# Issuing the down weights of the sorted experts from ScalarE instead of SyncE

## The reference

```
sel = exp_logits[group with the largest logit]        # 8 experts
ev, ei = top_k(softmax(sel), 2);  weights = group_p * ev / sum(ev)
for e in range(32):
    hid = silu(t @ w_expert_gate[e]) * (t @ w_expert_up[e])     # 1024 -> 256
    out = out + combine[:, e:e+1] * (hid @ w_expert_down[e])    # 256 -> 1024
return rms_norm(x + out, final_norm_gain)
```

## Time and profile before

| | us |
|---|---|
| median of 3 runs | 773.46 (772.38 to 773.94) |
| profiled execution | 772.11 |
| its span | 770.4 |
| PE busy | 698.3 (91%) |
| ACT busy | 289.1 (38%) |
| chain that ended last: PE | 83% |

### The profile page before, as it was taken

The page is one execution under the profiler, slowest core; times in us unless marked ns, Lnnn a source line. Parts: engine busy times, 40 slices in busy tenths (PEclk is TensorE's granted clock), DMA queues, the critical chain, the costliest instruction groups (busy, mean ns, idle before and its releaser), DMA issues.

```text
span 770.4 us, 10976 instructions
## 1 busy us (share of the span) xinstructions
PE 698.3 (91%) x4246; PEld 512.1 (66%) x4246; DVE 335.0 (43%) x614; ACT 289.1 (38%) x534; POOL 199.7 (26%) x171
## 2 busy tenths in 40 slices
PE   3999999998999999999999995699999999997840
PEld 3688888887878798888777885454454555554420
DVE  4349897979684423465478136500000000000008
ACT  6313645571444653555543032021222223131203
POOL 2045433431241231542452000212212121221110
PEclk9999999999999999999999996699999999999975
DMA  7913333030030030205841339999999999999726
GB/s 228 353 57 135 110 110 109 15 137 14 28 124 14 2 111 1 110 1 213 333 145 57 131 119 393 367 381 397 419 400 418 397 419 400 418 419 419 304 93 251
DMA packets 45122, 164.66 MB, mean 214 GB/s; under 512 B 9420, under 2 KB 13532, under 8 KB 32270
## 3 DMA queue, kind: packets, MB, share of 16 engines
q1 hardware_dynamic: 39758, 155.52, 52.1%
q0 software_dynamic: 5312, 8.42, 3.1%
HBM read 154.09 MB, written 19.53 MB: 225 GB/s over the span
## 4 chain that ended last, share of the span: by engine, by line
PE 83%; DVE 6%; ACT 4%; issue 3%; DMA 2%; POOL 1%; POOLq 0%; ACTq 0%; DVEq 0%
PE bank L970 14%; PE bank L472 13%; PE bank L474 13%; PE bank L473 13%; PE bank L1004 7%; PE bank L967 5%; PE bank L945 3%; PE bank L998 2%; PE bank L600 2%; PE bank L981 2%; DVE arena L2383 1%; PE bank L863 1%; PE bank L631 1%; PE bank L621 1%; PE bank L803 1%
## 5 line engine op out<-in xcount | busy, mean ns | idle before, releaser
L1258 POOL TENSOR_TENSOR w_lo<-arena,w_hi 128x1024 fp32r<-128x1024 f32 x36 | 86.0, 2395 | 209.4 <-ACT w_hi L1421 209.4
L472 PE MATMUL bank<-h_hi,w_hi 128*128 128x512 f32 x320 | 128.2, 401 | 0.4 <-DVE arena L1970 0.4
L474 PE MATMUL bank<-h_hi,w_lo 128*128 128x512 f32 x320 | 124.9, 390 | 0.0
L473 PE MATMUL bank<-h_lo,w_hi 128*128 128x512 f32 x320 | 124.6, 390 | 0.0
L970 PE MATMUL bank<-arena 128*64 128x256 f32 x896 | 107.1, 394 | 8.2 <-issue 7.4
L970 PEld LDWEIGHTS bank<-arena 128*64 128x64 f32 x896 | 66.5, 141 | 38.8 <-issue 8.6
L2337 DVE TENSOR_TENSOR arena<-arena,bank 64x256 f32<-64x256 f32 x28 | 11.6, 413 | 181.8 <-ACT arena L1772 181.8
L1882 DVE SCALAR_TENSOR_TENSOR bank<-arena,bank 128x512 f32<-128x512 f32 x116 | 78.7, 749 | 0.1
L1382 POOL DMA_INDIRECT y_rows<-arena,row_half x28 | 28.1, 1002 | 166.8 <-ACT arena L1793 155.5
L474 PEld LDWEIGHTS bank<-h_hi,w_lo 128*128 128x128 f32 x320 | 60.0, 188 | 13.1
L472 PEld LDWEIGHTS bank<-h_hi,w_hi 128*128 128x128 f32 x320 | 60.1, 188 | 12.9 <-DVE arena L1970 0.6
(11 more groups left out here) (358 smaller groups left out, 1128.2 us busy)
## 6 DMA issues: line engine op xcount, KB each, us to landing
arena<-in_w_expert_down_dram SPq DMA_DIRECT2D x33, 1024.0 KB
arena<-in_w_expert_gate_dram SPq DMA_DIRECT2D x33, 1024.0 KB
arena<-in_w_expert_up_dram SPq DMA_DIRECT2D x33, 1024.0 KB
arena<-in_w_in_dram SPq DMA_DIRECT2D x8, 2048.0 KB, 8.2
arena<-in_x_dram SPq DMA_DIRECT2D x8, 512.0 KB, 7.3
arena<-in_w_in_dram SPq DMA_DIRECT2D x4, 1024.0 KB, 10.3
y_rows<-arena SPq DMA_DIRECT2D x8, 512.0 KB, 10.4
arena<-in_w_out_dram SPq DMA_DIRECT2D x2, 2048.0 KB, 10.5
```

The source lines that it names most:

```text
L472: pe.matmul(o, wh, xh, start=first, stop=False)
L473: pe.matmul(o, wh, xl, start=False, stop=False)
L474: return pe.matmul(o, wl, xh, start=False, stop=last)
L1258: gp.tensor_tensor(as_raw(w_lo[pslot(s)], s), raw(s), as_raw(w_hi[pslot(s)], s).bitcast(F32), ALU.subtract)\
```

## The change

SP keeps the issue of gate and up and no longer waits for `ex_d`. The down weights of steps 6 to 32 are issued by ACT: in step i, behind the copy of the rows `ex_y(i - 1)`, it reads the expert's number of step i + 5 from `order_i` and issues that step's down weights on its own queue. `ex_y(i - 1)` has waited for the down matmuls of step i - 1, whose slot is overwritten.

```
-                wait(sp, "ex_d", outs(i))
-                expert_dn(s, e)
...
+            def down_load(s):
+
+                o = 0 if s == EXTRA else col_of[s]
+                e = act.value_load(order_i[0:1, o:o + 1], min_val=0, max_val=NE - 1)
+                act.dma_start(wd[slot_of(s)], a["w_expert_down"][0].rearrange("e (p m) n -> e p m n", m=JE)[e])\
+                    .then_inc(S[f"ld_d{slot_of(s)}"], 16)
...
                 if i > 0:
                     ex_y(i - 1)
+                    if i - 1 + NSLOT < NSTEP:
+                        down_load(steps[i - 1 + NSLOT])
```

## The result

The changed kernel takes 775.87 us in the median of 16 runs (773.45 to 779.7), the kernel before 773.23 us in as many. The ratio is 1.0053 with a 95% interval of 1.0039 to 1.0067: slower by 3.0 to 5.2 us, while the two medians lie 2.6 us apart. I had forecast +4.7 us. One run of the kernel before, at 837.25 us, was in a slow state of the chip and is left out of the ratio.

A forecast was written before the change was run, and what follows sets the result against it. DMA was taken to bound the tail. Four downs ahead (10.0 us) less 0.5 early gain delay steps 28 and 29; step 32's matmuls end at 741.4, not 736.71: +4.7 us, 776.8 (778.2 on the runs' scale), range 772.0 to 782.0.

The forecast's parts named there:

- The bytes and not the issue bound the tail: Steps 28 to 32: landing depends on bytes queued ahead, 2.50 us per down, not on when a transfer is issued.
- A second queue is served beside the first: ACT's queue takes turns with SP's, so a down lands a few us after issue while SP's gate and up wait.
- Four downs come ahead of gate and up: Steps 28 and 29: four downs newly ahead, 4 x 2.50 us less 0.5, landing at 709.1 and 717.6.
- early gain: Between 500 and 512 us, where the queue ran dry: gate and up issued sooner win 0.5 us, bounds 0 and 0.7.
- PE cannot catch up: After a 2.7 us wait before step 29, PE starts step 32 from work at 737.8, its matmuls taking 3.60 us.
- ACT's work is hidden: Between ex_y and hidT_copy: 0.8 us a step, 22 us in 27 steps, cost 0; without DMA cover 0.7 us.
- Rival C: ACT's issues of downs are held by the backlog, making hidT_copy late: 4 us on top, 782; chance 0.12.
- Rival A: DMA engines serve both queues by age, gate and up one down further ahead: gain 3.0 us, 770.5; chance 0.12.
- Rival B: Step 32's late landing is paid back by the clock, 1.76 us; +0.2 to +0.9 remain, 773.7 to 774.4; chance 0.18.

The follow-up runs named there:

- e6: Against the kernel before, ACT issues only the downs of steps 6 to 18, SP those of steps 19 to 32: 0.9968, -2.5 us.
- e8: Against the kernel before, SP issues the downs of steps 6 to 18, ACT those of steps 19 to 32: 1.0046, +3.6 us.
- e3: The changed kernel, but in step i ACT issues the down of step i + 3, not i + 5: 1.0048 against the kernel before, +3.7 us.
- e7: The changed kernel with ACT's lead five steps for the downs of steps 6 to 8, then three: 1.0030 against the kernel before, +2.3 us.
- e2: The kernel before, all transfers on SP's queue, each down issued behind the next step's gate and up: 0.9960, -3.1 us.
- e1: The changed kernel, but SP keeps its wait for ex_d, so gate and up are issued as late as before: 1.0078 against the kernel before, +6.0 us.
- e5: The kernel before, with two reads of the expert's number and a one-column activation added on ACT at 27 places, no transfer: 1.0002.
- e4: The kernel before, with a read of the expert's number and an unused 64-byte HBM-to-HBM transfer added on ACT at 27 places: 1.0155, +12.0 us.
- e11: The kernel before with each down issued on SP's queue behind the next step's gate and up, as in e2, measured again: 0.9961, -3.0 us.

## Why the prediction was right, and where not

- *The bytes and not the issue bound the tail.* Right: 410 GB/s in both kernels, and e6 against e8.
- *A second queue is served beside the first.* Right: 10.0 us to landing for a down on ACT's queue, 27.5 for `gain3` and 45.4 for step 24's up on SP's. The round of the queues that the Trainium skill describes agrees with that ("DMA: Bandwidth & Descriptors", "Queues, rings and completion order").
- *Four downs come ahead of gate and up, 10.0 us less the early gain.* Right that downs come ahead, too high for the steps it was worked out for. In the changed kernel SP's issues of the up weights of steps 28 and 29 and their landings are:

```profile
665.92 4.28 SPq L1141 DMA_DIRECT2D arena<-in_w_expert_up_dram  x1
...
DMA to landing us min/median/max: 41.5/41.5/41.5
```
```profile
674.04 8.01 SPq L1141 DMA_DIRECT2D arena<-in_w_expert_up_dram  x1
...
DMA to landing us min/median/max: 42.6/42.6/42.6
```

  They land at 707.42 and 716.64, or 216.1 and 225.3 from the first load, against 209.88 and 218.34 before: 6.2 and 7.0 us later where I had 9.5. ACT had issued downs 28 to 31 at 674.25, 690.58, 699.05 and 704.82. Each takes some 10 us to land, so when step 28's weights landed, down 31 was still under way: about three were ahead, not four. I had counted a down as ahead from its issue. At step 24, landing at 677.35, it was four: downs 24 to 27, issued at 646.33, 654.78, 660.66 and 667.47. The 9.33 us by which step 24 starts late look like my 9.5, but they are its delay of some 11 us less the reserve that PE had there (next point), and the likeness is luck. e3 and e7 do not prove that the number of downs ahead sets the delay.
- *PE cannot catch up.* Right, and step 32 starts out of work at the full clock (3.60 us), but the place was wrong. I had taken the stall before step 29 from the chain of before as the last that counts. After, it is the one before step 24, a broad step. I had looked only at the steps that had waited before, and step 24 had not: it had no wait, but less reserve than the delay: from e2's landing at 172.6 one can estimate 172.6 + 2.50 = 175.1 for the kernel before, 1.7 us ahead of its start, and a delay of some 11 us there became a stall. PE then needs 58.20 us to step 32 (677.48 to 735.68), and steps 28, 29 and 32 start at 711.35, 717.05 and 735.68 where I had 709.1, 717.6 and 737.8; 1.56 us of each measured start lie before the stage.
- *Early gain.* Mis-sized: 0.5, at most 0.7 us forecast; the transfers end 1.0 us sooner, the windows from 494 us on make it 1.8 us, and e1 against the changed kernel 1.9 us, within the noise. The bound came from the DMA share alone (0.96 against 1.02), which hides how much a busy engine moves: the GB/s in the same row, 352 against 410, would have given 12 x 58 / 410 = 1.7 us.
- *ACT's work is hidden.* Right: e5, 1.0002. Rival C did not occur; issues on ACT took 390 ns at most.
- *Rival A's order is a gain.* The order by age, made by hand in e2, gives -3.1 us where I had 3.0. The chip doesn't serve two queues so: ACT's downs landed 10.0 us after their issue, past a backlog on SP's queue that took 45.4 us.
- *Rival B, no net change, as the clock pays the late landing back.* The timed runs exclude it (at least +3.0 us). The profiled pair alone does not: its stage loses 1.0 us, near B's +0.9, and step 32 starts out of work as B had it.

The forecast is thus right in sign and in its mechanism. The timed runs also agree with its size, but that is in part luck: the landings at steps 28 and 29 were forecast 2.5 to 3.3 us too late, the stall came earlier than forecast, and in the profiled pair the stage loses only 1.0 us. Why seven of the 16 runs lie 4.2 us above the other nine (means 778.8 and 774.5) stays open.

## What to carry to other kernels

Where the DMA engines are full, a second issuing queue is a choice of priority, not bandwidth: what goes on it overtakes the backlog of the first. Keep in the order of use what one consumer needs in turn; issuing each load as soon as its buffer is free can be had on the one queue (e2). To find where a delay will bite, look for the step with the least reserve, not for the one that waits already.

## What the runs showed that I had not expected

Small transfers on a second queue can slow a full DMA. In e4, 27 transfers of 64 bytes between HBM addresses made 864 packets on q10, and the rate fell from 410 to 391 GB/s, 5%; the loss is 12.0 / 27 = 0.44 us for each:

```profile
520.00:718.00 198.00, 188.38 (x1074) 98.26 (x1072) 9.92 (x24) 48.17 (x108) 38.97 (x39) 0.97 1.01 391
```
```profile
q10 hardware_dynamic: 864, 0.00, 0.1%
```
That ACT's instructions are not the cause is shown by e5. Whether it is the transfers' size, their writes to HBM or their number was not tried.

The DMA share does not tell the rate: between 500 and 512 us it rose by 3% (0.96 to 0.99), the GB/s by 12% (352 to 396).

The clock of TensorE does not follow the length of the last wait alone. After a wait of 1.98 us step 32 began at the 1.2 GHz level in the kernel before (5.36 us; granted clock 0.51 in the earlier trace rows); after 1.96 us in e2 and, below, 1.98 us in e6 it ran at 2.4 GHz (3.67 us, granted clock 1.00 from 730 to 734 us). It isn't a property of the kernel either: e11 is e2 once more, and its profile, the second below, has 5.36 us again. So 1.7 us of what the profiles of e2 and e6 gain on the one before are this; in the timed runs e2 and e11 gain the same (0.9960 and 0.9961).

```profile
728.29 1.98 issue
730.27 3.67 PE bank L970 x32
```
```profile
726.58 1.98 issue
728.56 5.36 PE bank L970 x32
```
